# A mixture-of-experts decoder block: all 24 weight pieces of an expert step in split precision

## The reference

```
gu = xc @ w_gate_up[e] + b_gate_up[e]          # 128 rows of tokens; 1024 x 2048
g = min(gu[:, :1024], 7);  u = clip(gu[:, 1024:], -7, 7)
act = (u + 1) * (g * sigmoid(1.702 * g))
y = act @ w_down[e] + b_down[e]                # 1024 x 1024
out[token] += y * slot_weight
```

## Time and profile before

| | us |
|---|---|
| runs of the kernel before | 2251.74, 2253.74, 2250.10 (median 2251.74) |
| the profiled execution | 2247.22 |
| its span, first to last instruction | 2245.6 |
| mean granted PE clock | 0.971 |
| PE busy in the span | 2109.2 (94%) |
| DVE busy | 1491.8 (66%) |
| ACT busy | 1195.0 (53%) |
| mean DMA rate | 218 GB/s |

### The profile page before, as it was taken

One profiled execution on the slowest core, in us unless ns is written; L12 is line 12 of the kernel. 1 busy time (PEld: TensorE's weight loads), 2 busy tenths in 40 slices (PEclk: granted clock), 3 DMA queues, 4 the chain that ended last, 5 costly groups with the idle time before them and its releaser, 6 DMA issues.

```text
span 2245.6 us, 35483 instructions
## 1 busy us (share of the span) xinstructions
PE 2109.2 (94%) x11224; PEld 1474.1 (66%) x11225; DVE 1491.8 (66%) x1900; ACT 1195.0 (53%) x1623; POOL 282.7 (13%) x334
## 2 busy tenths in 40 slices
PE   7989988999989669999999999999999999999993
PEld 4445555767668547777777677776777777776772
DVE  4326654555444557877877668977877887876784
ACT  3152434334333336666756557766665766765674
POOL 3010000000002410110222101111211010210000
PEclk9999999999999779999999999999999999999997
DMA  7110020110043576987977779978979979976994
GB/s 224 38 38 0 22 75 1 38 38 19 20 169 113 157 228 227 353 297 277 371 271 255 245 280 380 373 261 285 355 252 332 370 264 375 345 256 242 373 344 158
DMA packets 247678, 489.51 MB, mean 218 GB/s; under 512 B 19915, under 2 KB 29991, under 8 KB 247536
## 3 DMA queue, kind: packets, MB, share of 16 engines
q1 hardware_dynamic: 218768, 439.37, 54.2%
q0 software_dynamic: 21088, 49.35, 8.3%
q10 hardware_dynamic: 7776, 0.19, 0.2%
HBM read 461.01 MB, written 32.05 MB: 220 GB/s over the span
## 4 chain that ended last, share of the span: by engine, by line
PE 90%; DVE 4%; issue 3%; DMA 1%; SPq 1%; ACT 1%; POOL 0%; POOLq 0%; ACTq 0%; DVEq 0%
PE psum L659 15%; PE psum L660 14%; PE psum L663 14%; PE psum L676 8%; PE psum L427 5%; PE psum L552 5%; PE psum L650 5%; PE psum L540 3%; PE psum L542 3%; PE psum L535 3%; PE psum L642 2%; PE psum L451 2%; PE psum L495 2%; PE psum L621 2%; PE psum L597 1%
## 5 line engine op out<-in xcount | busy, mean ns | idle before, releaser
L1463 DVE TENSOR_TENSOR w_lo<-ring,w_hi 128x1024 fp32r<-128x1024 f32 x704 | 850.3, 1222 | 162.8 <-ACT w_hi L900 142.1
L900 ACT ACTIVATE w_hi<-ring 128x1024 fp32r<-128x1024 f32 x704 | 741.0, 1061 | 349.2 <-PE psum L663 337.4
L659 PE MATMUL psum<-w_hi,rows_hi 128*128 128x512 f32 x896 | 372.1, 415 | 4.2 <-DVE rows_lo L1467 2.7
L660 PE MATMUL psum<-w_hi,rows_lo 128*128 128x512 f32 x896 | 350.4, 391 | 0.0
L663 PE MATMUL psum<-w_lo,rows_hi 128*128 128x512 f32 x896 | 277.0, 390 | 0.0
L659 PE MATMUL psum<-w_hi,act_hi 128*128 128x512 f32 x512 | 220.0, 430 | 0.3 <-issue 0.3
L659 PEld LDWEIGHTS psum<-w_hi,rows_hi 128*128 128x128 f32 x896 | 169.5, 189 | 52.2 <-issue 20.9
L660 PE MATMUL psum<-w_hi,act_lo 128*128 128x512 f32 x512 | 202.4, 395 | 0.0
L663 PEld LDWEIGHTS psum<-w_lo,rows_hi 128*128 128x128 f32 x896 | 168.5, 188 | 36.2
L660 PEld LDWEIGHTS psum<-w_hi,rows_lo 128*128 128x128 f32 x896 | 169.2, 189 | 32.9
L676 PE MATMUL psum<-ring,region_m 128*32 128x256 f32 x3072 | 174.2, 380 | 0.0
(11 more groups left out here) (289 smaller groups left out, 2747.8 us busy)
## 6 DMA issues: line engine op xcount, KB each, us to landing
ring<-in_w_gate_up_dram SPq DMA_DIRECT2D x128, 2048.0 KB, 14.9
ring<-in_w_down_dram SPq DMA_DIRECT2D x64, 2048.0 KB, 11.4
ring<-in_w_in_dram SPq DMA_DIRECT2D x9, 1024.0 KB, 8.1
ring<-in_w_in_dram SPq DMA_DIRECT2D x3, 2048.0 KB, 22.8
region_m<-in_x_dram SPq DMA_DIRECT2D x8, 512.0 KB, 9.8
ring<-in_w_out_dram SPq DMA_DIRECT2D x2, 2048.0 KB, 7.6
region_a<-in_x_dram POOLq DMA_DIRECT2D x8, 512.0 KB, 4.7
acc_rows<-region_a POOLq DMA_DIRECT2D x8, 512.0 KB, 2.9
```

Of the source, the lines that this page charges most:

```text
L659: mm(bank(i), hi[:, ks], wh, start=(k0 + q == 0), stop=False)
L660: mm(bank(i), lo[:, ks], wh, start=False, stop=False)
L900: act.activation(w_hi[:, (m + u * NSP) % NBUF, :], place[i][:, k0 * HALF:(k0 + 2) * HALF], ACT.Copy).then_inc(hi_done, 1)
L1463: v.tensor_tensor(out=w_lo[:, buf, :], in0=place[i][:, k0 * HALF:(k0 + 2) * HALF], in1=w_hi[:, buf, :].bitcast(f32), op=ALU.subtract).then ...
```

## The change

Pieces 7 and 15 become split pieces like the others; `NATIVE`, `SPLIT`, `NSP` and `rows_f` go, and every piece n now has buffer n % 4 and the semaphore count of its own number. The high and the low part of activation half 1 are made after piece 20 in place of piece 21, on ACT and on DVE. PE turns the next step's rows in every step, with no `If` around it; in the last step, where there is no next one, it waits for a count that has been reached and transposes rows that nobody reads.

```diff
-NATIVE = (7, 15)
-SPLIT = tuple(n for n in range(SUBS) if n not in NATIVE)
-NSP = len(SPLIT)
...
-        rows_f = take(2 * P)
...
                         def piece(n):
 
                             i, k0 = sub_unit(n)
-                            if n in NATIVE:
-                                for q in range(2):
-                                    last = mm(bank(i), rows_f[:, q * P:(q + 1) * P], wu[i][:, k0 + q, :], start=False, stop=False)
-                            else:
-                                m = SPLIT.index(n)
-                                buf = (m + u * NSP) % NBUF
-                                hi, lo = (rows_hi, rows_lo) if i < 4 else (act_hi, act_lo)
-                                pe.wait_ge(hi_done, j * NSP + m + 1)
-                                for q in range(2):
-                                    ks = slice((k0 + q) * P, (k0 + q + 1) * P)
-                                    wh = w_hi[:, buf, q * HALF:(q + 1) * HALF]
-                                    mm(bank(i), hi[:, ks], wh, start=(k0 + q == 0), stop=False)
-                                    mm(bank(i), lo[:, ks], wh, start=False, stop=False)
-                                pe.wait_ge(lo_done, j * NSP + m + 1)
-                                for q in range(2):
-                                    last = mm(bank(i), hi[:, (k0 + q) * P:(k0 + q + 1) * P], w_lo[:, buf, q * HALF:(q + 1) * HALF],
-                                              start=False, stop=False)
-                                last.then_inc(sub_mm, 1)
+                            buf = n % NBUF
+                            hi, lo = (rows_hi, rows_lo) if i < 4 else (act_hi, act_lo)
+                            pe.wait_ge(hi_done, j * SUBS + n + 1)
+                            for q in range(2):
+                                ks = slice((k0 + q) * P, (k0 + q + 1) * P)
+                                wh = w_hi[:, buf, q * HALF:(q + 1) * HALF]
+                                mm(bank(i), hi[:, ks], wh, start=(k0 + q == 0), stop=False)
+                                mm(bank(i), lo[:, ks], wh, start=False, stop=False)
+                            pe.wait_ge(lo_done, j * SUBS + n + 1)
+                            for q in range(2):
+                                last = mm(bank(i), hi[:, (k0 + q) * P:(k0 + q + 1) * P], w_lo[:, buf, q * HALF:(q + 1) * HALF],
+                                          start=False, stop=False)
+                            last.then_inc(sub_mm, 1)
                             if k0 + 2 == KD:
                                 if i == 0:
                                     pe.wait_ge(sel_ready, j + 1)
...
                                     tail_product(bank(1)[:, 0:QC], (0, 2), rows_of).then_inc(tgate_mm, 1)
                                     tail_product(bank(0)[:, 0:QC], (1, 3), rows_of).then_inc(tup_mm, 1)
                             if n == NEXT_ROWS_AT:
-                                with pe.If(more > 0):
-                                    wait_reg(pe, rows_in[1 - u], (pair + 1 + u) * 16)
-                                    rows_turn(1 - u)
+                                wait_reg(pe, rows_in[1 - u], (pair + u + more) * 16)
+                                rows_turn(1 - u)
                             if n == TAIL_ACT_AT:
                                 with pe.If(tail > 0):
                                     wait_reg(pe, tact_done, before + 1)
...
-                act.activation(rows_f, bank(7)[:, 2 * P:4 * P], ACT.Copy)
-            def high(m, u, j):
-
-                i, k0 = sub_unit(SPLIT[m])
+            def high(n, j):
+
+                i, k0 = sub_unit(n)
-                act.wait_ge(sub_mm, j * NSP + m + 1)
-                act.activation(w_hi[:, (m + u * NSP) % NBUF, :], place[i][:, k0 * HALF:(k0 + 2) * HALF], ACT.Copy).then_inc(hi_done, 1)
+                act.wait_ge(sub_mm, j * SUBS + n + 1)
+                act.activation(w_hi[:, n % NBUF, :], place[i][:, k0 * HALF:(k0 + 2) * HALF], ACT.Copy).then_inc(hi_done, 1)
-            for m in range(NBUF):
-                high(m, 0, 0)
+            for n in range(NBUF):
+                high(n, 0)
...
-                            if n == 21:
+                            if n == 20:
                                 actT_out(1)
                         with act.If(tail > 0):
                             wait_reg(act, tactT_mm, before + 1)
...
-            def low(m, u, j):
-
-                i, k0 = sub_unit(SPLIT[m])
-                buf = (m + u * NSP) % NBUF
-                dve.wait_ge(hi_done, j * NSP + m + 1)
-                v.tensor_tensor(out=w_lo[:, buf, :], in0=place[i][:, k0 * HALF:(k0 + 2) * HALF],
-                                in1=w_hi[:, buf, :].bitcast(f32), op=ALU.subtract).then_inc(lo_done, 1)
+            def low(n, j):
+
+                i, k0 = sub_unit(n)
+                dve.wait_ge(hi_done, j * SUBS + n + 1)
+                v.tensor_tensor(out=w_lo[:, n % NBUF, :], in0=place[i][:, k0 * HALF:(k0 + 2) * HALF],
+                                in1=w_hi[:, n % NBUF, :].bitcast(f32), op=ALU.subtract).then_inc(lo_done, 1)
...
                                     tail_glu_part()
-                            if n == 21:
+                            if n == 20:
                                 actT_low(1)
                         with dve.If(more > 0):
                             dve.wait_ge(rowsT_done, j + 2)
                             rows_low()
-                            for m in range(NBUF):
-                                low(m, 1 - u, j + 1)
+                            for n in range(NBUF):
+                                low(n, j + 1)
                         dve.nop()
```

More of the change, by code:

```diff
@@ L928, in output @@
                                            scale=meta[:, u, 1:2].bitcast(f32)).then_inc(y_done, 1)
-                        for m in range(NBUF, NSP):
-                            n = SPLIT[m]
-                            high(m, u, j)
+                        for n in range(NBUF, SUBS):
+                            high(n, j)
                             if n == 8:
@@ L953, in _ @@
                             rowsT_out()
-                            high(0, 1 - u, j + 1)
+                            high(0, j + 1)
                         wait_reg(act, added, j * 16 + 16)
@@ L957, in _ @@
                         with act.If(more > 0):
-                            high(1, 1 - u, j + 1)
-                            high(2, 1 - u, j + 1)
+                            high(1, j + 1)
+                            high(2, j + 1)
                         output(1)
                         with act.If(more > 0):
-                            high(3, 1 - u, j + 1)
+                            high(3, j + 1)
                         with act.If(tail > 0):
@@ L1472, in _ @@
             rows_low()
-            for m in range(NBUF):
-                low(m, 0, 0)
+            for n in range(NBUF):
+                low(n, 0)
             with dve.Fori(0, MAXS // 2) as pair:
@@ L1511, in actT_low @@
                                             op=ALU.subtract).then_inc(act_lo_done, 1)
-                        for m in range(NBUF, NSP):
-                            n = SPLIT[m]
-                            low(m, u, j)
+                        for n in range(NBUF, SUBS):
+                            low(n, j)
                             if n == 4:
```

## The result

| | before | changed |
|---|---|---|
| median of the runs, us | 2251.72 (6 runs) | 2230.74 (6 runs) |
| lowest to highest | 2250.10 to 2253.74 | 2228.41 to 2232.28 |
| profiled execution, us | 2247.22 | 2231.87 |

The changed kernel takes 0.9905 of the time before, 95% interval [0.9892, 0.9918]: 21.0 us less, where 20.7 were forecast (2231.0 us). The interval reaches from 18.5 to 24.3 us, so that the two agree to 0.3 us is luck; that they agree within 3 us is not.

The account below looks back on a forecast made before the run. PE was taken to set the pace, with DVE close behind. T steps -18.6 us, N steps -2.4, last step +0.6 and start -0.3 made -20.7, from 2251.7 to 2231.0 us; range 2214 to 2249.

Parts of the forecast that it names:

- The saving: Pieces 7 and 15 on PE: 1.36 us split, 1.72 native, so 0.70 us less work in all 32 steps.
- The gap: Ahead of the row transposes on PE: 0.46 us, counted from `act_lo`, gone in T steps, just hidden in N steps.
- The chain: PE ahead of piece 18 in each N step: waits 1.0 us for DVE's work up to `act_done`, bounds 0 and 3.1.
- The sum: 16 T steps -18.6 us, 15 N steps -2.4, last step +0.6, once ahead of the loop -0.3: together -20.7 us.
- B: No wait at piece 18: N steps gain 1.16 us too, 16 us more, 2215 us; chance 0.12.
- C: Gap at piece 20 stays, caused by the wait with a computed count: 14.3 us come back, 2245 us; chance 0.14.
- D: DVE later, from low 9 to `act_done`, as ACT releases parts late: N step loses 2.3 us more, 2268 us; chance 0.09.
- E: Transfers become the bound in N steps: rate sagging 2.5% gives 38.3 us, 16 us more, 2247 us; chance 0.03.

Follow-up runs that it names:

- e4: Kernel before, pieces 7 and 15 native, with only activation half 1 converted after piece 20 and no `If` around the row turn: 2234.08 us, ratio 0.9934.
- e5b: Changed kernel, DVE's up part 1 ahead of low part 18 and PE's wait for `act_lo` half 1 behind the row turn: 2211.14 us, ratio 0.9833.
- e2: Changed kernel with the `If` around the row turn put back: 2228.99 us, ratio 0.9913.
- e3: Changed kernel with activation half 1 converted after piece 21 again, no `If`: 2251.41 us, ratio 1.0011.
- e1: Changed kernel with activation half 1 converted after piece 21 again and the `If` around the row turn put back: 2254.09 us, ratio 1.0022.
- e7: Changed kernel with three more small DVE instructions, computing nothing used, after low part 13: 2233.16 us, ratio 0.9930.
- e5a: Changed kernel with DVE doing up part 1 ahead of low part 18: 2226.82 us, ratio 0.9911.
- e6: Changed kernel with PE waiting for `act_lo` half 1 behind the row turn: 2227.62 us, ratio 0.9907.

## Why the prediction was right

**The saving.** Split pieces take 1.36 us (1.37 at piece 7) where native ones took 1.72, as put. From e4 to e5b, where nothing waits, the N step goes from 36.88 to 36.21 and the T step from 49.36 to 48.65: 0.67 and 0.71 us, against 0.70.

**The gap.** Its size and that it would just be hidden in N steps were right, and so was its cause, a late `act_lo` behind which PE's queue still has the branch and the row wait to work out (e2, e3). The close meeting forecast for N steps came about: `act_lo` is done at 1803.94, the transposes start at 1804.43, and PE is ready for them at 1803.96 + 0.46 = 1804.42. The figure of the Trainium skill (Advanced Engine Details and Errata, Control Flow Timing), some 108 ns for a compare-and-branch, is no part of the step's time here: with the branch back, T steps are equal to 0.01 us. It shows only where the wait ahead of it binds, as the 0.1 us of the N steps in e2 and of all steps between e3 and e1, and there the trace agrees with it.

**The chain.** Forecast: PE waits 1.0 us in each N step; measured 0.90. The working put `act_done` 19.57 us behind the conversion of piece 8, and it came 19.60 behind (1801.07 - 1781.47). Two errors of about 0.2 us cancel. ACT's timeline, with the conversions of pieces 8 and 9:

```profile
1781.47 1.07 ACT L889 ACTIVATE w_hi<-ring 128x1024 fp32r<-128x1024 f32 x1 [0.55 <-PE psum L654]
...
1782.92 1.05 ACT L889 ACTIVATE w_hi<-ring 128x1024 fp32r<-128x1024 f32 x1
```

ACT started piece 9's conversion 1.45 us after piece 8's and not 1.61, sooner after the sigmoid than the trace of before let one see, since there it waited for PE at that point; and DVE had the small pauses that e7 shows. That the sum came out to 0.03 us was luck; each half alone would have moved the N steps by 0.2 us and the total by 3 us. The range of 0 to 3.1 us that I gave this term was right to be wide.

**The sum.** The terms are met step by step: T steps -1.17 us (forecast -1.16), N steps -0.19 (forecast -0.16). The loop, from the first L1467 to the last (1358.6 us before, 1338.4 us from the first L1454 to the last), is 20.2 us shorter. What comes after the last of them is 0.87 us longer (forecast 0.6, the turn of rows that nobody reads), and from the first row transposes to the first `rows_lo`, where the copy `rows_f` stood, it is 0.28 us shorter (forecast 0.3). The first step is 0.55 us longer, 36.86 against 36.31; in the other kernels' profiles it lies between 35.6 and 37.7 us, so this says nothing of the change. The profiled execution of the changed kernel reached the loop 4.0 us later than that of before; in the other kernels' profiles the same point lies between 807.9 and 810.8 us. I take this for scatter, since 2.2 us of it are a longer wait for the first rows' transfer (25.6 against 23.4 us) and 1.4 us lie in earlier waits for DVE (L410, 14.8 against 13.4 us).

**The rivals.** B (no wait at piece 18) is out by the 16 waits. C falls by e2. D needed 1.3 us more per N step; there was none. E, the transfers: the same N step's rate went from 367 to 373 GB/s in the changed kernel and 374 in e5b, with DMA share 1.05, and no engine waited for weights. The 367 was no ceiling before the change either, as another N step of the kernel before shows:

```profile
1394.22:1431.59 37.37, 37.08 (x163) 28.14 (x162) 33.37 (x35) 27.52 (x31) 3.45 (x3) 1.00 1.05 377
```

E was also priced a little low: 38.3 us against the 37.2 forecast is 1.1 us, and 18 us in 16 steps, not 16. The Trainium skill's figure for a core's share of the memory, about 358 GB/s (DMA: Bandwidth & Descriptors, Specifications), did not bind here: two N steps in a row of the changed kernel ran at 377 and 376 GB/s. In e5b the same two took 36.2 us each at the same rates. How much further the rate would go no run here shows.

## What to carry to other kernels

Work moved off the busiest engine is worth what the next engine leaves of it, and that is decided between two waits and not over the step: DVE was at 89% of an N step before the change and at 94% after it, yet it was late by 0.9 us at one point, because its extra work lay in one stretch ahead of that point. Walk the second engine's instructions from the place where it last was idle to the one that the first engine waits for; that took four rows of start times and came within 0.1 us of the wait, in part because two errors of 0.2 us cancelled. And look whether two waits are fed by the same queue: taking one away alone moves the time to the other (e5a, e6), and only both together give it back.

## What the runs showed of the hardware

A conditional that PE enters in each step cost nothing measurable when the wait ahead of it was met early (T steps of 48.65 us with and without it, e2), and 0.1 us when it was not.

What stands between a wait and the first product behind it is added to a late wait. From the end of the DVE instruction that PE waits for to that product there were 0.56 to 0.62 us with the branch and the row wait in between (T steps of the kernel before and N steps of e1), 0.44 to 0.49 us with the row wait alone (e3), and 0.05 us at L678, where nothing stands in between (1801.07 to 1801.12). Where `act_lo` was done 1.27 us ahead, in the T steps of the changed kernel, none of it showed.
